# Decoder trunk: the sum of squares ahead of the embedding gate moves to VectorE for the first token half, and the inverse roots are taken on turned 32-column blocks

## The reference, cut to what matters

```
h = h + rmsnorm_post(ConvFFN(...))                       # "down" stage and its residual
h = h + sigmoid(rmsnorm(h, g_ple) @ w_gate) * (p @ w_proj)   # "ple" and "pw" stages
rmsnorm(x, g) = x / sqrt(mean(x*x) + 1e-6) * g
```

## Time and profile before

| | |
|---|---|
| median of 3 runs | 1294.93 us (1294.84 to 1295.06) |
| the profiled execution, its time | 1294.98 us |
| its span | 1293.2 us |
| TensorE matmuls busy | 1285.8 us, 99% |
| VectorE busy | 890.7 us, 69% |
| ScalarE busy | 593.6 us, 46% |
| GpSimd busy | 75.5 us, 6% |
| granted TensorE clock | full in all 40 slices (2.4 GHz) |

### The profile page before, as it was taken

The page is one execution under the profiler, slowest core; times in us unless marked ns, Lnnn a source line. Parts: engine busy times, 40 slices in busy tenths (PEclk is TensorE's granted clock), DMA queues, the critical chain, the costliest instruction groups (busy, mean ns, idle before and its releaser), DMA issues.

```text
span 1293.2 us, 25224 instructions
## 1 busy us (share of the span) xinstructions
PE 1285.8 (99%) x10762; PEld 1252.6 (97%) x10762; DVE 890.7 (69%) x1602; ACT 593.6 (46%) x1060; POOL 75.5 (6%) x114
## 2 busy tenths in 40 slices
PE   9999999999999999999999999999999999999998
PEld 8999989999999999999999978999999999999998
DVE  7899776887777774223897788688777777422485
ACT  5214565554444443223755777554444444222381
POOL 1112230000100000000031020000000000000000
PEclk9999999999999999999999999999999999999999
DMA  5535621313342333222314232311332323322231
GB/s 197 155 101 191 202 99 51 106 58 104 96 107 86 95 109 115 90 90 78 133 54 159 66 99 81 115 50 52 97 94 87 98 85 108 114 90 91 79 130 67
DMA packets 35616, 131.84 MB, mean 102 GB/s; under 512 B 4516, under 2 KB 5260, under 8 KB 35184
## 3 DMA queue, kind: packets, MB, share of 16 engines
q1 hardware_dynamic: 29664, 111.33, 27.0%
q0 software_dynamic: 5408, 18.26, 4.4%
q10 hardware_dynamic: 432, 0.64, 0.2%
HBM read 121.26 MB, written 10.08 MB: 102 GB/s over the span
## 4 chain that ended last, share of the span: by engine, by line
PE 98%; DVE 1%; ACT 0%; issue 0%; POOL 0%; DVEq 0%; POOLq 0%
PE tile L1171 24%; PE tile L1175 24%; PE tile L1173 24%; PE tile L1181 5%; PE tile L1182 5%; PE tile L1183 5%; PE side L1181 1%; PE side L1182 1%; PE side L1183 1%; PE tile L1643 1%; PE side L1666 1%; PE sums L1220 0%; PE side L1306 0%; PE sums L1681 0%; PE sums L1342 0%; PE sums L1688 0%
## 5 line engine op out<-in xcount | busy, mean ns | idle before, releaser
L749 ACT ACTIVATE wH<-raw 128x1024 fp32r<-128x1024 f32 (+1 forms) x190 | 210.9, 1113 | 379.3 <-DMA raw<-in_w_up 148.2
L1171 PE MATMUL tile<-xH,wH 128*128 128x260 f32 x1798 | 363.0, 283 | 0.0
L1175 PE MATMUL tile<-xH,wL 128*128 128x260 f32 x1798 | 362.7, 283 | 0.0
L1173 PE MATMUL tile<-xL,wH 128*128 128x260 f32 x1798 | 362.1, 283 | 0.0
L1813 DVE TENSOR_TENSOR wL<-raw,wH 128x1024 fp32r<-128x1024 f32 (+1 forms) x190 | 245.8, 1294 | 153.6 <-ACT wH L749 149.5
L1171 PEld LDWEIGHTS tile<-xH,wH 128*128 128x128 f32 x1798 | 277.1, 189 | 3.5 <-issue 3.0
L1175 PEld LDWEIGHTS tile<-xH,wL 128*128 128x128 f32 x1798 | 277.3, 189 | 0.0
L1173 PEld LDWEIGHTS tile<-xL,wH 128*128 128x128 f32 x1798 | 276.4, 188 | 0.0
L1861 DVE SCALAR_TENSOR_TENSOR u<-tile,rstd 128x520 f32<-128x520 f32 x96 | 67.1, 699 | 119.8 <-PE tile L1175 119.6
L1171 PE MATMUL tile<-hidH,wH 128*128 128x260 f32 x616 | 124.4, 283 | 0.0
L1175 PE MATMUL tile<-hidH,wL 128*128 128x260 f32 x616 | 123.9, 282 | 0.0
(11 more groups left out here) (429 smaller groups left out, 1892.7 us busy)
## 6 DMA issues: line engine op xcount, KB each, us to landing
raw<-in_w_up SPq DMA_DIRECT2D x88, 512.0 KB, 3.6
raw<-in_w_down SPq DMA_DIRECT2D x32, 704.0 KB, 4.0
raw<-in_w_ple SPq DMA_DIRECT2D x16, 512.0 KB, 5.6
raw<-in_w_qo SPq DMA_DIRECT2D x12, 512.0 KB, 3.6
raw<-in_w_qkv SPq DMA_DIRECT2D x12, 512.0 KB, 3.6
raw<-in_w_kv SPq DMA_DIRECT2D x10, 512.0 KB, 3.7
cring<-in_c_in POOLq DMA_DIRECT2D x8, 512.0 KB, 4.8
out_c_s<-cring POOLq DMA_DIRECT2D x8, 512.0 KB, 3.2
```

The costliest lines, as they stand in the source:

```text
L749: nc.scalar.activation(wH[j][:, 0:n], raw[j][:, 0:n], ACT.Copy).then_inc(s_high, 1)
L1171: nc.tensor.matmul(out[:, q, 0:HT], wh, x[0][:, k, tokens(q)], start=first, stop=False)
L1173: nc.tensor.matmul(out[:, q, 0:HT], wh, x[1][:, k, tokens(q)], start=False, stop=False)
L1175: mm = nc.tensor.matmul(out[:, q, 0:HT], wl, x[0][:, k, tokens(q)], start=False, stop=last)
```

## The change

For token half 0 of the gate, in both layers, `square_group` and `group_sums` go away. VectorE adds the eight tiles of squares to one in four additions (`fold_embedding_squares`), one after each of the steps 0 to 3 of token half 1: two over 520 columns that add four tiles to four, one over 520 that makes two of them, one over 260 that makes one. TensorE sums that tile with one matmul, now inside the third chunk, after its tile k = 0. ScalarE takes the root after `ple_input(4, 1)` and not after `ple_input(2, 1)`. In token half 1, `square_group` and `square_sum` each stand one tile k later.

Every inverse of a root becomes `invert`: a transpose of 32 x 32 blocks, RECIPROCAL on the few columns that the blocks leave over, RECIPROCAL on one column of each block, and a transpose that reads this column again and again. The number is the same on all partitions, so that one column of a turned block holds the 32 tokens of the block.

```diff
-GROUPED = {sq: n + 1 for n, sq in enumerate(sq for sq in PREROOT if sq[0][:2] != "up" or sq[1])}
+FOLDED = {sq: n + 1 for n, sq in enumerate(sq for sq in PREROOT if sq[1] == 0)}
+GROUPED = {sq: n + 1 for n, sq in enumerate(sq for sq in PREROOT if sq[1] == 1)}
...
                 high(ple, 1)
                 ple_input(0, 1)
-                group_sums(ple, 0)
                 p_copy(6)
                 high(ple, 2)
                 ple_input(1, 1)
                 p_copy(7)
-                ple_input(2, 1)
+                for k in range(2, 5):
+                    ple_input(k, 1)
                 pre_root(ple, 0)
-                ple_input(3, 1)
-                for k in range(4, KT):
+                for k in range(5, KT):
                     ple_input(k, 1)
...
-                    if j == 5:
-                        square_group(ple, 0, 0)
-                        square_group(ple, 0, 1)
 
                 yd = YREAD0[down]
-                square_sum(ple, 0)
                 first_half(ple, 0, (s_yr, yd + KT - 1))
                 first_half(ple, 1, (s_pwr, 2 * KT * (layer + 1)))
-                first_half(ple, 2, (s_pwr, 2 * KT * (layer + 1)))
-                for k in range(3):
+                first_half(ple, 2, (s_pwr, 2 * KT * (layer + 1)), lambda k: square_sum(ple, 0) if k == 0 else None)
+                for k in range(4):
                     for c in range(SPLIT):
                         second_half(ple, c, k, k + 1)
                 square_group(ple, 1, 0)
                 square_group(ple, 1, 1)
                 for c in range(SPLIT):
-                    second_half(ple, c, 3, 4)
+                    second_half(ple, c, 4, 5)
                 square_sum(ple, 1)
                 for c in range(SPLIT):
-                    second_half(ple, c, 4, KT)
+                    second_half(ple, c, 5, KT)
...
+            def invert(rows, scratch):
+
+                blocks = rows.shape[-1] // 32
+                whole = 32 * blocks
+                blocked, turned = (t[:, 0:whole].rearrange("p (b t) -> p b t", t=32) for t in (rows, scratch))
+                column = turned[:, :, 0:1]
+                chain.did(nc.vector.transpose(turned, blocked))
+                chain.did(nc.vector.reciprocal(rows[:, whole:], rows[:, whole:]))
+                dve.wait_ge(s_dve, chain.n)
+                chain.link(nc.vector.reciprocal(column, column))
+                chain.link(nc.vector.transpose(blocked, column.to_broadcast([P, blocks, 32])))
+
-            def one_over(stage, q, dst):
+            def one_over(stage, q, dst, scratch):
                 dve.wait_ge(s_root, ROOT[stage, q])
-                chain.link(nc.vector.reciprocal(dst, dst))
+                invert(dst, scratch)
...
+            def fold_embedding_squares(stage, part):
+
+                half = KT // 4
+                tiles = square(stage, 0, 0), square(stage, 0, 1)
+                if part < 2:
+                    early, late = sg[part], squares_ple[:, half * part:half * part + half, :].rearrange("p k t -> p (k t)")
+                    dve.wait_ge(s_sq, SQ0[stage] + KT)
+                    chain.did(nc.vector.tensor_tensor(early, early, late, ALU.add))
+                    return
+                dve.wait_ge(s_dve, chain.n)
+                if part == 2:
+                    chain.did(nc.vector.tensor_tensor(sg[0], sg[0], sg[1], ALU.add))
+                else:
+                    nc.vector.tensor_tensor(tiles[0], tiles[0], tiles[1], ALU.add).then_inc(s_fold, 1)
...
-                one_over(down, 1, cg[:, tokens(1)])
+                one_over(down, 1, cg[:, tokens(1)], rstd[:, tokens(1)])
                 for k in range(KT + 2):
                     step(k, 1)
+                    if k < 4:
+                        fold_embedding_squares(ple, k)
                     if k in (1, 3, 4):
                         low(ple, {1: 0, 3: 1, 4: 2}[k])
```

More of the change, by code:

```diff
@@ L1230, in square_sum @@
                     pe.wait_ge(s_root, ROOT[POST[stage], q])
-                    pe.wait_ge(s_fold, int(stage[2]) + 1)
+                    pe.wait_ge(s_fold, FOLDED[stage, q])
                 nc.tensor.matmul(sums[:, q, 0:HT], ones, square(stage, q, 0), start=True, stop=True).then_inc(s_squ, 1)
@@ L1814, in low @@
                                         ALU.subtract).then_inc(s_low, 1)
-            def one_over(stage, q, dst):
+            def invert(rows, scratch):
[9 more added lines that the diff above has]
+            def one_over(stage, q, dst, scratch):
                 dve.wait_ge(s_root, ROOT[stage, q])
-                chain.link(nc.vector.reciprocal(dst, dst))
+                invert(dst, scratch)
             def pre_one_over(stage, q):
                 dve.wait_ge(s_rootp, PREROOT[stage, q])
-                chain.link(nc.vector.reciprocal(rstd[:, tokens(q)], rstd[:, tokens(q)]))
+                invert(rstd[:, tokens(q)], cg[:, tokens(q)])
             def fold_squares(stage, q):
@@ L1919, in _ @@
             low("kv", 3)
-            one_over("kv", 0, rstd[:])
+            one_over("kv", 0, rstd[:], cg[:])
             fg, ig, ea = u[0:NH, 0, 0:T], cv[0:NH, :], u[0:NH, 1, 0:T]
@@ L2198, in feed_forward @@
                 step = residual(mixer, up, y, layer, G_POST_MIX, G_PRE_FFN)
-                one_over(mixer, 0, cg[:, tokens(0)])
+                one_over(mixer, 0, cg[:, tokens(0)], rstd[:, tokens(0)])
                 step(0, 0)
@@ L2222, in feed_forward @@
                 dve.wait_ge(s_pad, layer + 1)
-                one_over(mixer, 1, cg[:, tokens(1)])
+                one_over(mixer, 1, cg[:, tokens(1)], rstd[:, tokens(1)])
                 for k in range(KT + 2):
@@ L2290, in feed_forward @@
                 step = residual(down, ple, y_down, layer, G_POST_FFN, G_PLE)
-                one_over(down, 0, cg[:, tokens(0)])
+                one_over(down, 0, cg[:, tokens(0)], rstd[:, tokens(0)])
                 for k in range(KT + 2):
@@ L2559, in _ @@
                     low("qkv", 2)
-                    one_over("qkv", 0, rstd[:])
+                    one_over("qkv", 0, rstd[:], cg[:])
                 scaled_read("qkv", c, vs[:, c, :] if c < 2 else u[:, c % 2, 0:T], scale=QK_SCALE if c >= 4 else 1.0)
```

## The result

The changed kernel takes 1297.22 us (median of 19 runs, 1296.98 to 1297.66), the kernel before 1294.9 us in the same comparison. The ratio is 1.0018, with a 95% interval of 1.0012 to 1.0024. It is slower by 2.3 us, where I forecast 3.4. The profiled execution's span grew from 1293.2 to 1295.3 us, 2.1 us.

What follows compares the result with a forecast made beforehand. TensorE's matmuls, busy 1285.8 of 1293.2 us, were taken as the bound. Per layer, chunk 1 1.26 us late plus 0.44 for the moved sum gave 1.70, twice 3.40: 1298.4 us; eight-in-ten range 1296.7 to 1300.1.

Steps and rivals of the forecast that it cites:

- The mechanism: Gate, each layer: additions delay VectorE's low weights, so TensorE idles about 1.3 us before chunk 0 and 1.5 us before chunk 1.
- The other inverses: Inverses outside the gate stretch: they get shorter too, but TensorE is not waiting there, so counted as 0 us.
- My sum of 3.40 us: Whole kernel: 1.70 us later per layer, twice, added to the profiled execution's 1294.98 us.
- The inverse: VectorE ahead of gate chunk 0: new inverse takes 1.38 us for 1.81, starts later, so 0.33 us won.
- a layer's shift: Gate's second halves start 1.70 us later: chunk 1 late by 1.26 us plus 0.44 for the moved sum; bounds 1.56 to 2.7.
- The size of the wait at chunk 0: Gate, after the products: TensorE waits 1.3 us, from about 627.6 us, for low weights ending at 628.88.
- The repeated read: Last transpose of the inverse, reading one column 32 times: forecast no extra cost; slow-read rival 1298.8 us, chance 0.05.
- The rule of the Trainium skill: Last transpose of the inverse: non-adjacent reads lose about 0.65 cycle per element, some 0.17 us longer, kernel 0.35 us; chance 0.05.
- the half-way rival: Gate: VectorE's steps overlap better than added up, giving 1296 to 1297.5 us; chance 0.18 together with the full no-change form.

## Why the prediction was right in kind and off in size

- **The mechanism held.** Two additions ahead of each of the first two low weights, TensorE waiting at chunk 0 and chunk 1 for `wL`, no wait at the moved sum or ahead of chunk 3: all as predicted. Moving the additions takes the loss away and leaving them out does no more, so this part is shown. From the start of the first low weights to that of the second I had 4.38 us; it took 631.30 - 626.94 = 4.36.
- **The step that failed:** "The other inverses get shorter too; at each TensorE is not waiting, so I count nothing for them." At two places of a layer it was waiting, 0.28 and 0.29 us, 1.14 us in all: with the inverses alone the span is 1.1 us shorter, and so it is with just those two. One wait stood in the earlier trace rows; the other was hidden under overlapping records and shows only in the distance of starts. With this term most of the miss is explained. My sum of 3.40 us, less 1.14, less 2 x 0.13 for the smaller shift at the gate (the next two points), and 0.11 more for what arises at 184 us, makes 2.1 us, the growth of the span.
- **The inverse was sized too long.** I had 1.38 us and a loss of 0.10 us on top, since a transpose would start after the instruction ahead had ended. It took 1.25 us, and the transpose started 0.08 us before that instruction's end (623.32 against 622.91 + 0.49). RECIPROCAL over 4 columns took 0.14 us, not the 0.17 of the earlier trace rows. So the low weights of chunk 0 start 4.03 us after the anchor at 622.91, where I had 4.27 (627.66 - 623.39).
- **A restart has a price that I left out.** Behind a wait the second matmul starts 0.23 us after the first (632.58 to 632.81) in place of 0.12. From the start of chunk 1 to the second halves I had 637.81 + 1.70 - 633.31 = 6.20 us; it took 638.90 - 632.58 = 6.32. So a layer's shift was 1.57 us where I had 1.70: earlier low weights took off 0.25 us, and 0.12 came back, most of it at this restart.
- **The size of the wait at chunk 0** was 1.3 us in my text. The start came 0.91 us after the last product, 0.79 more than the usual 0.12 from start to start. Counted from the step that waited for `xH`, the low weights were earlier, and the products ended later, because a copy of ScalarE's held one up by 0.26 us (0.38 from 624.08 to 624.46 in place of 0.12), which I had not seen. It changes nothing in the sum, as the run with the low weights first shows: chunk 1 decides.
- **The repeated read** costs nothing. The groups of VectorE by line and shape, with the mean in ns behind the bar:

```profile
L1822 DVE STREAM_TRANSPOSE rstd<-cg 128x256 f32<-128x256 f32 x8 | 3.6, 446 | 0.3
...
L1818 DVE STREAM_TRANSPOSE rstd<-cg 128x256 f32<-128x256 f32 x8 | 3.6, 444 | 9.1 <-ACT cg L760 9.1
```

446 ns with the column repeated 32 times, 444 ns with a plain read. The rule of the Trainium skill that I had weighed as a rival (page "Vector Engine (DVE) Microarchitecture Reference", section 5.2, on the access granule) would, by my estimate from it, have made it some 170 ns longer; the trace does not agree.
- **The range held partly by luck.** 1297.22 us lies below what my own sum gave with its bounds (1298.1 to 1300.4). It lies in the wider range (from 1296.7) only because I had reached down to the half-way rival (1296 to 1297.5). That rival holds the measured time, but not by its reason: VectorE's row did not overlap better by a microsecond; its low weights of chunk 1 came 0.25 us earlier than I had reckoned, and nearly all of that is the inverse.

## What to carry to other kernels

When an engine's list is the bound and another engine feeds it, cost a step by its place in the feeder's row and look for the last deadline it stands ahead of; the same additions cost 4.2 us ahead of the low weights and nothing behind them. When an instruction gets shorter everywhere, go through the bound engine's starts near every use, by the distance of starts rather than by idle time, before counting nothing. Work taken off the bound engine may have covered small waits; here over half of the group's 1.21 us came free only when a copy and a low weight were moved as well.

## What the hardware showed that I had not expected

- A 128x256 transpose whose source has a step of zero takes as long as a plain one, 446 and 444 ns, and the first transpose of the inverse started 0.08 us before the instruction ahead had ended. The late starts in the earlier trace rows are therefore not a property of the transpose in general.
- A TensorE that has waited starts its second matmul 0.11 us later than one in a running row (0.23 us in place of 0.12), at each of the two waits of the gate in a layer. The two late starts of the kernel without additions show the same (0.22 and 0.23 us).
